# PEER routing on one Trainium2 core: a second fold and a subtraction go to GpSimd, VectorE's sum per pick has 13 numbers in place of 25

## What is computed

```python
q = (hf @ w_q).reshape(T, PEER_HEADS, 2, PEER_HALF)
s1 = jnp.einsum('thd,hkd->thk', q[:, :, 0], sub_keys[:, 0])
s2 = jnp.einsum('thd,hkd->thk', q[:, :, 1], sub_keys[:, 1])
v1, i1 = lax.top_k(s1, PEER_TOPK)
v2, i2 = lax.top_k(s2, PEER_TOPK)
cand = (v1[..., :, None] + v2[..., None, :]).reshape(T, PEER_HEADS, PEER_TOPK * PEER_TOPK)
sc, ci = lax.top_k(cand, PEER_TOPK)
e = (jnp.take_along_axis(i1, ci // PEER_TOPK, axis=-1) * N_KEYS
     + jnp.take_along_axis(i2, ci % PEER_TOPK, axis=-1))
g = jax.nn.softmax(sc.astype(jnp.float32), axis=-1).astype(h.dtype)
```

## Time and profile before

| | |
|---|---|
| median of 3 runs | 1839.83 us (1839.45 to 1846.52) |
| the profiled execution | 1839.72 us, its span 1837.9 us |
| busy in the span | TensorE 93%, VectorE 85%, ScalarE 41%, GpSimd 37% |
| mean granted TensorE clock | 0.967 of full |

### The profile page before, as it was taken

One profiled execution on the slowest core, in us unless ns is written; L12 is line 12 of the kernel. 1 busy time (PEld: TensorE's weight loads), 2 busy tenths in 40 slices (PEclk: granted clock), 3 DMA queues, 4 the chain that ended last, 5 costly groups with the idle time before them and its releaser, 6 DMA issues.

```text
span 1837.9 us, 28650 instructions
## 1 busy us (share of the span) xinstructions
PE 1703.8 (93%) x9232; PEld 1400.1 (76%) x9232; DVE 1562.6 (85%) x3155; ACT 747.4 (41%) x1621; POOL 677.0 (37%) x610
## 2 busy tenths in 40 slices
PE   6999989979893788699999999999999999999998
PEld 4666765545552678588999999999898999999996
DVE  2687950177898999699999999999999999999999
ACT  3122561030000788444444444444444444444443
POOL 0000000005556888243434444444444444443441
PEclk9999999989986799899999999999999999999999
DMA  8443102111111468999999999999999999999996
GB/s 314 140 149 125 47 4 69 57 35 58 57 34 57 138 184 241 345 386 397 397 408 399 400 408 395 403 409 395 398 403 390 406 396 405 408 386 402 407 402 216
DMA packets 128780, 508.69 MB, mean 277 GB/s; under 512 B 8528, under 2 KB 63568, under 8 KB 79312
## 3 DMA queue, kind: packets, MB, share of 16 engines
q0 software_dynamic: 36864, 268.45, 36.3%
q1 hardware_dynamic: 91568, 239.34, 35.1%
q10 hardware_dynamic: 288, 0.13, 0.0%
HBM read 479.97 MB, written 27.92 MB: 276 GB/s over the span
## 4 chain that ended last, share of the span: by engine, by line
DVE 34%; PE 22%; DMA 21%; issue 19%; POOL 2%; ACT 1%; DVEq 1%; POOLq 0%; SPq 0%; ACTq 0%
DMA slab<-table,ixr 21%; PE psum L409 12%; DVE slab L1376 8%; DVE ulo L1292 4%; DVE slab L1330 3%; PE psum L410 3%; DVE slab L1368 2%; DVE vlo L1355 2%; PE psum L683 2%; DVE slab L1363 2%; DVE wlo L1351 1%; POOL slab L1456 1%; DVE slab L1334 1%; PE psum L546 1%; PE psum L397 1%
## 5 line engine op out<-in xcount | busy, mean ns | idle before, releaser
L1456 POOL DMA_INDIRECT slab<-table,ixr x256 | 424.9, 1660 | 604.3 <-DVE slab L1376 554.6
L409 PE MATMUL psum<-slab 128*128 128x512 f32 x624 | 329.7, 611 | 16.9 <-ACT slab L752 10.9
L704 PE MATMUL psum<-hhi,uhi 128*128 128x384 f32 x1008 | 339.1, 336 | 6.6 <-issue 6.5
L1376 DVE SCALAR_TENSOR_TENSOR slab<-slab,cf 128x1024 f32<-128x1024 f32 x256 | 328.2, 1282 | 14.7
L1368 DVE SCALAR_TENSOR_TENSOR slab<-slab,h2tok 128x1024 f32<-128x1024 f32 x256 | 312.0, 1219 | 31.7 <-DMA slab<-table,ixr 31.5
L704 PE MATMUL psum<-hhi,ulo 128*128 128x384 f32 x1008 | 338.2, 335 | 0.0
L704 PE MATMUL psum<-hlo,uhi 128*128 128x384 f32 x1008 | 337.6, 335 | 0.0
L718 PE MATMUL psum<-vhi,whi 128*128 128x512 f32 x768 | 299.9, 391 | 14.5 <-DVE wlo L1351 14.1
L718 PE MATMUL psum<-vhi,wlo 128*128 128x512 f32 x768 | 302.3, 394 | 0.0
L718 PE MATMUL psum<-vlo,whi 128*128 128x512 f32 x768 | 302.0, 393 | 0.0
L410 PEld LDWEIGHTS psum<-slab 128*128 128x128 f32 x624 | 120.7, 193 | 154.5 <-issue 154.5
(11 more groups left out here) (185 smaller groups left out, 2517.5 us busy)
## 6 DMA issues: line engine op xcount, KB each, us to landing
slab<-ublk SPq DMA_DIRECT2D x64, 1024.0 KB, 9.1
slab<-vtab SPq DMA_DIRECT2D x64, 1024.0 KB
slab<-wblk SPq DMA_DIRECT2D x90, 512.0 KB, 4.2
slab<-g_dram SPq DMA_DIRECT2D x32, 768.0 KB, 9.2
g_dram<-slab SPq DMA_DIRECT2D x11, 2048.0 KB, 8.8
slab<-table,ixr POOLq DMA_INDIRECT x256, 9.9
x<-x_in SPq DMA_DIRECT2D x1, 2560.0 KB, 9.6
y_out<-x SPq DMA_DIRECT2D x5, 512.0 KB, 3.5
```

Of the source, the lines that this page charges most:

```text
L409: pe.matmul(dst[:, 0:512], w, src[:, l0:l0 + T_L], start=start, stop=stop)
L704: last = pe.matmul(psum[:, b, 0:ND], w[:, c, :], m[:, c, :], start=(m_ == 0), stop=(m_ == 3 * DC - 1))
L1376: v.scalar_tensor_tensor(out=accs[k][:, e, :], in0=rows[:, sl % GR, D:2 * D], scalar=cf[:, sl:sl + 1], in1=accs[k][:, e, :], op0=ALU.mult, ...
L1456: pool.indirect_dma_start(out=rows[:, sl % GR, :], out_offset=None, in_=table, in_offset=bass.IndirectOffsetOnAxis(ap=ixr[:, half, sl % 8: ...
```

## The change

GpSimd adds, for each tile, the lower 12 of the 25 half sums onto the upper 12, in place, so that 13 numbers are left for a pick. VectorE's reduces L1198 and L1338 take those 13. The subtraction of the best value moves from VectorE to GpSimd, in between the candidates' numbers and the wait for `found`; VectorE signals it by `top_set`, and waits for the last one (`top_shifted`) before it overwrites `top`. ScalarE's exponential waits for the eighth subtraction in place of `shifted`.

```diff
+HALF = CAND // 2
+LEFT = HALF - HALF // 2
...
-HEAD_STEPS = 2 * 5 * TILES + len(RUNS) + 5 * TILES + 2
+HEAD_STEPS = 2 * 5 * TILES + len(RUNS) + 5 * TILES + 1
...
-            act.wait_ge(shifted, 1)
+            act.wait_ge(top_shifted, PH)
             act.activation(ex, ex, ACT.Exp).then_inc(exped, 1)
...
                 v.wait_ge(folded, i * TILES)
-                v.tensor_reduce(ef[:, :, bass.ds((i - 1) * TOP, TOP)], half, AX_X, ALU.add).then_inc(looked, 1)
+                v.tensor_reduce(ef[:, :, bass.ds((i - 1) * TOP, TOP)], half[:, :, :, HALF - LEFT:HALF], AX_X, ALU.add).then_inc(looked, 1)
...
                 own()
+                if not first:
+                    v.wait_ge(top_shifted, i)
+                    hold()
                 for t in range(TILES):
                     tk(v.max(top[:, t, 0:8], cand[:, t, :]))
...
-                tk(v.tensor_tensor(ex[:, :, bass.ds(i, 1), :].rearrange("p t a k -> p t (a k)"), top[:],
-                                   top[:, :, 0:1].broadcast_to([P, TILES, TOP]), ALU.subtract))
                 own()
+                v.sem_inc(top_set, 1)
...
             with v.Fori(1, PH) as i:
                 search(i, False)
-            v.wait_ge(topk_step, PH * HEAD_STEPS + 1)
-            v.sem_inc(shifted, 1)
...
-                    v.tensor_reduce(ef[:, 0:N_GATHER, (PH - 1) * TOP:PH * TOP], half_last, AX_X, ALU.add)\
+                    v.tensor_reduce(ef[:, 0:N_GATHER, (PH - 1) * TOP:PH * TOP], half_last[:, :, :, HALF - LEFT:HALF], AX_X, ALU.add)\
                         .then_inc(looked, 1)
...
+                pool.wait_ge(top_set, i + 1)
+                part = slice(i, i + 1) if tiles < TILES else bass.ds(i, 1)
+                pool.tensor_tensor(ex[:, :, part, :].rearrange("p t a k -> p t (a k)"), top[:], top[:, :, 0:1].broadcast_to([P, TILES, TOP]), ALU.subtract)\
+                    .then_inc(top_shifted, 1)
                 pool.wait_ge(number_step, (i + 1) * NUMBER_STEPS)
                 pool.wait_ge(found, i + 1)
                 for t in range(tiles):
                     pool.tensor_tensor(hit[:, t], place[:, t], eid[:, t, :].unsqueeze(2).broadcast_to([P, CAND, TOP]), ALU.mult).then_inc(valued, 1)
                     pool.wait_ge(valued, i * TILES + (t + 1))
-                    pool.tensor_tensor(half[:, t].rearrange("p k n -> p n k"), hit[:, t, 0:CAND // 2], hit[:, t, CAND // 2:CAND], ALU.add).then_inc(folded, 1)
+                    pool.tensor_tensor(half[:, t].rearrange("p k n -> p n k"), hit[:, t, 0:HALF], hit[:, t, HALF:CAND], ALU.add).then_inc(half_set, 1)
+                    pool.wait_ge(half_set, i * TILES + (t + 1))
+                    pool.tensor_tensor(half[:, t, :, LEFT:HALF], half[:, t, :, LEFT:HALF], half[:, t, :, 0:HALF - LEFT], ALU.add).then_inc(folded, 1)
```

More of the change, by code:

```diff
@@ L247, in build @@
         centred = sem("centred"); yscaled = sem("yscaled"); y_ready = sem("y_ready"); sk_done = sem("sk_done"); sk_read = sem("sk_read")
-        shifted = sem("shifted"); exped = sem("exped"); picked = sem("picked"); found = sem("found"); looked = sem("looked")
-        ranked = sem("ranked"); folded = sem("folded"); number_step = sem("number_step"); valued = sem("valued"); h2_tp = sem("h2_tp")
+        exped = sem("exped"); picked = sem("picked"); found = sem("found"); looked = sem("looked")
+        ranked = sem("ranked"); folded = sem("folded"); half_set = sem("half_set"); top_set = sem("top_set"); top_shifted = sem("top_shifted"); number_step = sem("number_step"); valued = sem("valued"); h2_tp = sem("h2_tp")
         h2_tok = sem("h2_tok"); dve_step = sem("dve_step"); topk_step = sem("topk_step"); paced = sem("paced")
```

## The result

| | before | changed |
|---|---|---|
| median of 20 runs | 1841.98 us (1839.45 to 1849.55) | 1848.58 us (1845.32 to 1854.19) |
| ratio to before | | 1.0034, 95% interval 1.0026 to 1.0042 |
| the profiled execution | 1839.72 us, span 1837.9 | 1848.45 us, span 1846.6 |
| busy VectorE, GpSimd | 1562.6, 677.0 us | 1568.8, 702.1 us |

The change makes the kernel 0.34% slower, some 6.3 us, where the forecast was +4.5 us and the range 1831 to 1850.

The account below looks back on a forecast made before the run. VectorE's own list was taken to bound the routing. Heads 1 to 7 give -6.7 us, collisions +12.6, head 0, L1338 and the tail -1.4: together +4.5, forecast 1844.3 us, range 1831 to 1850.

Parts of the forecast that it names:

- the collision: Heads 2 to 7: VectorE's seven candidate sums wait for GpSimd's last product and folds, 2.1 us late each, +12.6 in all.
- the tail: After head 7: L1306 ends 0.95 us earlier; GpSimd's list, 1.2 us longer, hides, or costs 1 us without cover.
- the likeliest case: Interleaved collision, GpSimd getting in between VectorE's sums: chance 0.58, own range 1842 to 1847 us for folds of 0.52 to 0.65.
- The short reduce: VectorE's L1198 over 1040 elements takes 1.23 us, 1.00 less, in seven turns; L1338 in the last head 0.40 less.
- The signals: VectorE's gaps around the moved subtraction: -0.15 + 0.09 ahead of the reduce, +0.09 ahead of L1246, +0.04 us in all.
- GpSimd's subtraction: On GpSimd behind top_set: 0.33 us a head, covered by VectorE's reduce, cast and compare, so nothing is paid.
- The second fold: GpSimd's added fold of 192 elements a tile: 0.58 us, bounds 0.45 and 1.04; a tile takes 3.27 us.
- once: Rival at the candidate sums: VectorE waits 0.92 us for the product, then keeps GpSimd out; 1837.2 us, chance 0.12.
- no collision: Rival: L1306's length is its own, from its broadcast operand, and the engines do not block; -8.1 us, 1831.7, chance 0.14.
- the dear fold: Rival: GpSimd's second fold takes 1.04 us, candidate sums come 4.1 us late; +16.5 us, 1856, chance 0.12.
- Six turns: Heads 2 to 7 of the routing loop: collision of 2.1 us each against VectorE's list 0.96 us shorter.
- L1306's 0.95 us: In the tail, L1306 waits 0.4 us for a short second fold in place of 1.35 for a product, ending 0.95 earlier.

Follow-up runs that it names:

- the subtraction alone: Kernel before with only the subtraction moved to GpSimd, one fold and the sum of 25 as before; ratio 1.0002 to before, turn 25.01 us.
- the late fold: Changed kernel, but GpSimd's second fold of all five tiles is one instruction, one head later; ratio 0.9965 to before, turn 23.95 us.
- the folds alone: Changed kernel with the subtraction put back on VectorE, second folds and short reduce kept; ratio 1.0037 to before, turn 26.22 us.
- the spare work: Kernel before plus a GpSimd addition of 192 elements a tile that nobody reads; ratio 1.0069 to before, turn 27.19 us.

## Why the prediction was right

The time was forecast at +4.5 us and measured at +6.3, with the mechanism of the collision as told, but one step, in the tail, wrong. The median of 1848.58 us lies in the range of 1831 to 1850, but above the 1842 to 1847 given for the likeliest case, though the second fold took 0.59 us, well inside the 0.52 to 0.65 of that case. Of this, 2.2 us are the starting point: 20 runs put the kernel before at 1841.98 and not at 1839.83. The other 1.8, by the ratio, are an error of the sum. By its steps:

- *The short reduce*: 1.23 forecast, 1.24 measured; L1338's of 416 elements, 0.57 for 0.57.

```profile
L1340 DVE TENSOR_REDUCE ef<-slab x1: 571/571/571, 660.9 to 660.9; 128x32 f32<-128x416 f32 x1
```

- *The signals*: +0.04 forecast; the gap ahead of L1251 grew by 0.12 (0.14 to 0.26) and the reduce comes 0.44 behind the last search in place of 0.48, so +0.08. With the subtraction alone, +0.06 a turn.
- *GpSimd's subtraction*: nothing forecast, nothing found.
- *The second fold*: 0.58 forecast, 0.59 measured; a tile each 3.29 us for 3.27.
- *The collision*: 2.1 us a head forecast, 2.25 measured, and shown as the cause by the late fold (gone), the folds alone and the spare work (there in full). The waits on the product, the fold and the second fold are 1.00, 0.85 and 0.40 us, which is all of the 2.25; the first was put at 0.92. The cast adds nothing, since the sums of before had lost as much to it. There the forecast misread the rows a little: it took GpSimd to be free at 539.70, where a cast of 0.34 us starts 0.08 later, and 1.01 us to be the sums' own length, which is 0.83. Head 1 was spared, as forecast. The rivals "once" and "no collision" are out by the single sums, the dear fold by its 0.59.
- *Six turns*: 6 x (2.1 - 0.96) = 6.8 forecast, 6 x (2.25 - 0.92) = 8.0 by the measured terms, 7.92 in the trace.
- *The tail* is the step that failed. L1306's 0.95 us came as forecast (2.16 to 1.21). But that GpSimd's longer list would hide was worked out only from what waits for GpSimd by semaphore. The memset, put by the forecast itself at about 612.1 for its end, met two VectorE instructions that stood at 611.17 before and were to come 1.95 earlier. It shares no data with them, and held them 1.64 us. From the last reduce to the first hot row -1.95 was forecast and -0.37 measured. Taking the memset away gave back 1.56 there; where it was put instead it held up other instructions for 1.07.

Of the 1.8 us by which the sum was low, the collision and the signals account for 1.1 in the six turns, which the trace shows. The memset is 1.6 more in the trace up to the first hot row. The two together are 2.7, more than the 1.8; the difference is within the noise of the ratio, 1.5 us either way, so the whole time can't confirm the size of the memset's part. The range was 19 us wide and this step worth 1.6, so that the time fell into the range says nothing for the tail.

## What to carry to other kernels

Before work is moved to an idle engine, lay the two timelines side by side: on VectorE and GpSimd it matters which instructions meet, not how much each has to do. GpSimd had 10 us to spare in a turn and only 0.44 at the place that counted; the same folds, beside VectorE's one-input searches, turned 0.34% slower into 0.35% faster. A blocked instruction shows as a long one and as busy time, so compare its length with that of a like one where the other engine is idle, and look also at what slides later without anybody waiting for it. When something is moved out of the way, look at what it meets at its new place.

## What the runs showed that was not expected

- A GpSimd memset, which reads nothing, left VectorE's two-input f32 additions alone (0.83 us for seven), but held two one-input uint32 instructions of 128 elements (L1319, L1320) for 1.64 us, to its end; without it they took 0.22. At its new place it held an instruction of L1332, f32 with one tensor input, in the same way (1.73 us).
- A collision does not hold up only the first of a chain. With 0.1 us between VectorE's sums, each GpSimd instruction that came up got in between two of them: four waits in seven instructions.
- Whether a short or a long GpSimd instruction stood ahead of VectorE's softmax weights hung, in the two traces with the same code there, on 0.6 us of ScalarE's time: 1.22 or 2.17 us.
- The candidate sums lost some 0.18 us a head to a cast of GpSimd in the kernel before already, though GpSimd seemed to be out of their way.
